# Odd layer's scan: one form of the inverse as TensorE's transpose of the other, carried products in other levels, output weights requested earlier

## The chip, the cores and the metric

One Trainium2 chip, one of its cores. The metric is the device time of one launch in microseconds (us), lower is better. The kernel runs one inference step of a two-layer backbone in float32. TensorE (PE) multiplies matrices into PSUM, VectorE (DVE) and ScalarE (ACT) work on vectors and move results from PSUM to SBUF, GpSimd (POOL) and SyncE (SP) mostly issue DMAs here.

## The reference, cut to what matters

The backbone has an even layer (mLSTM and latent attention) and an odd layer (an SSD scan and a gated delta rule, here GDN), each followed by a mixture of experts. The change touches only the scan of the odd layer and what stands just behind it:

```python
def gdn_scan(q, k, v, beta, g, S0):
    # chunked gated delta rule, log-decay gc = cumsum(g)
    amat = eye(L) + dec_strict * (kc @ kc.T) * bc          # unit lower triangular
    u0 = triangular_solve(amat, vc)
    w  = triangular_solve(amat, exp(gc) * kc)
    pmat = dec_incl * (qc @ kc.T) * bc
    def step(S, xs):
        u = u0i - wi @ S
        o = exp(gi) * (qi @ S) + pi @ u
        S = exp(gl) * S + (exp(gl - gi) * bi * ki).T @ u
        return S, o

def odd_mixer(h, P, oi, ctx):
    y = h @ P['w_in_odd'][oi]
    ...
    ys = rms_norm(ys * silu(z_s), P['ssd_norm'][oi])        # SSD output, 512 wide
    og = rms_norm(of + flip_t(ob), P['gdn_norm'][oi]) * silu(z_g)   # per head of 128
    out = concatenate([ys, og], -1) @ P['w_out_odd'][oi]
```

There are 384 tokens (128 of a prompt, 256 of a sample), in three tiles of 128; both directions are scanned, with 4 GDN heads and 8 SSD heads.

## The kernel before, in words

**Units and pairs.** `scan_units` (line 153) lists six units, a direction d and a token tile c each: (0,0), (1,0), (0,1), (1,2), (0,2), (1,1). They run in three pairs, pair 0 to pair 2; below, a and b are the two units of a pair. Pairs 1 and 2 carry a state in (`sequence`), pairs 0 and 1 hand one on (`moves_on`). All work of one unit is 128 rows by 512 columns: four heads of 128 by 128.

**The inverse.** Each unit needs the inverse of its unit triangular matrix. It is built in six levels, from blocks of one up to blocks of 64. It is kept in two forms: `XT`, and its transpose `X`. `AT` is the matrix, and `level(n)` on DVE (L2407) cuts from it the blocks `LT` of level n. In each level n of 1 to 6 (L1438 to L1482 on PE):

- `T1` = LT and X multiplied (PE, L1447 by the helper L1015), copied from PSUM to `TT` by ACT (L1820);
- `XT` product = TT and XT multiplied (PE), subtracted from `XT` by DVE (L2466);
- `XX` product = XT and TT multiplied the other way round (PE), subtracted from `X` by DVE (L2469); not in level 6, since X is not needed after it.

The helper `four` issues one product for each of four heads. The first `X` of a pair is a transpose of `XT` on PE (`X0`, L1433), copied by ACT (L1816).

**What stands between.** Between T1 and the two products of a level other work of the pair is issued: in levels 1 and 2 `Es` (the decays of the SSD part, spread by PE, L1010; exponentials on ACT, L1805) and `GB` (one product a unit, L1448); in level 3 `Y1` (SSD output of the tile itself, L1454); in level 4 `Y2` (SSD output of the carried state, L1462); in level 5 `HU` (the next SSD state, L1468); in level 6 `KS` (k times the carried GDN state) and `O2` (q times it). Behind level 6 come `U` (the solve), `O1` (output) and `SU` (next GDN state).

**Order and banks.** Each engine executes its instructions in the order in which the program writes them. `plan_jobs` (line 173) lists every PSUM user as a job, and job number modulo 8 is its bank. Thus a job waits, beside its inputs, until the job eight before it in this list has been read (`issue`, L877). PE's program has to issue the jobs in just this order.

**Buffers.** The buffers of the scan lie in four parts of 4096 words: one carved from the arena, and the three slots of the weight `ring`. Unit a has the arena part and slot 0, unit b slots 1 and 2.

**Behind the scan.** DVE multiplies the SSD sum `ysum` by its gate (L2508, `odd_sums`). ACT squares and sums it (L1835), takes a root (L1836), squares the 12 pieces of the GDN sum `ogsum` (L1839) and takes their roots (L1841). DVE scales both (L2515, L2522), PE transposes them (`mT`, L1522), ACT copies them (L1844), and `project_out` multiplies with `w_out_odd`. SP requests the two halves of `w_out_odd` (2 MB each, ring slots 1 and 2) when the first `odd_sums` is done (L583 of `load`, the DMA at L611), and behind them on its queue the small shift rows (L672) and the first experts of the next stage (L638).

## Time and profile before

| | |
|---|---|
| median of 3 runs | 1511.68 us (1505.21 to 1513.31) |
| the profiled execution's own time | 1506.36 us |
| its span, first to last instruction | 1504.2 us |
| mean granted TensorE clock | 0.940 of full |
| PE busy | 88% of the span |
| odd layer's scan, first T1 of pair 0 to O1 of pair 2 | 914.5 to 1124.0 us of the span |

The profiled execution is 5.3 us below the median; 2.2 us of its time lie outside the span. In the profile PE is TensorE's matmul side and PEld its weight loads; "[x <-DVE ...]" behind a row is the idle time ahead of it and what ended it. A float32 product of TensorE stands as two records in the trace and a transpose as one, so `four` is a group of 8 records and four transposes one of 4.

### The profile page before, as it was taken

The page shows a single profiled execution, that of the slowest core. Times are in us where ns is not written, and L with a number is a line of the kernel's source. Part 1 is how long each engine was busy: PE and PEld are TensorE (multiplying, and loading weights), DVE is VectorE, ACT ScalarE, POOL GpSimd, SP SyncE. Part 2 cuts the span into 40 slices and gives each one's busy share as a digit, 9 for nine tenths or more (in the row PEclk, how much of TensorE's full clock was granted, in tenths as well). Part 3 has the DMA queues.
Part 4 walks back from the last instruction along what each step waited for, and adds up shares of the span by engine and source line. Part 5 has one row for each costly group of instructions (what it writes and reads, how often), then busy time and mean ns, then how long its engine had stood idle before and what let it go on. Part 6 is the DMA issues. An engine that isn't in the chain of part 4 may idle for free.

```text
span 1504.2 us, 17094 instructions
## 1 busy us (share of the span) xinstructions
PE 1316.4 (88%) x6506; PEld 815.0 (54%) x6506; DVE 527.8 (35%) x1090; ACT 339.2 (23%) x724; POOL 112.3 (7%) x136
## 2 busy tenths in 40 slices
PE   6999788999998997888999997978877989987883
PEld 3554675466884333333565557878776843333332
DVE  3010473332234111011557817677662341101014
ACT  2100314333231111111336213221223311111111
POOL 2400010000001111110000000000000011111100
PEclk9999897999999999999999999999797999999997
DMA  9951666166537999997342200100007379999971
GB/s 362 332 180 58 223 152 246 68 238 240 222 139 296 390 415 418 418 417 311 122 152 72 85 0 1 29 1 1 1 18 287 137 294 411 413 418 418 417 287 63
DMA packets 80726, 329.12 MB, mean 219 GB/s; under 512 B 18383, under 2 KB 19577, under 8 KB 55936
## 3 DMA queue, kind: packets, MB, share of 16 engines
q1 hardware_dynamic: 66224, 300.54, 51.3%
q0 software_dynamic: 14416, 27.41, 5.7%
q8 instruction: 56, 0.92, 0.3%
q14 instruction: 30, 0.25, 0.0%
HBM read 320.04 MB, written 29.53 MB: 232 GB/s over the span
## 4 chain that ended last, share of the span: by engine, by line
PE 63%; DMA 15%; DVE 13%; issue 6%; ACT 2%; SPq 0%; POOL 0%; DVEq 0%; ACTq 0%; POOLq 0%
PE psum L921 20%; PE psum L1266 12%; PE psum L1015 9%; DMA arena<-in_moe_w_up 6%; PE psum L1292 5%; PE psum L947 3%; DMA wide<-in_moe_w_up 3%; DMA ring<-in_moe_w_up 3%; PE psum L1010 2%; DMA ring<-in_ada_w 2%; DVE arena L2381 2%; DVE wide L2341 1%; PE psum L890 1%; DMA arena<-h_rows,slot_token 1%; PE psum L954 1%
## 5 line engine op out<-in xcount | busy, mean ns | idle before, releaser
L921 PE MATMUL psum<-wide,ring 128*128 128x384 f32 x704 | 240.6, 502 | 3.8 <-ACT wide L1580 1.9
L921 PEld LDWEIGHTS psum<-wide,ring 128*128 128x128 f32 x704 | 165.6, 239 | 70.9 <-issue 9.5
L1266 PE MATMUL psum<-arena 128*64 128x512 f32 x480 | 151.6, 624 | 19.0 <-DMA ring<-in_moe_w_up 11.7
L1266 PE MATMUL psum<-ring,arena 128*64 128x512 f32 x384 | 134.4, 624 | 8.9 <-DMA wide<-in_moe_w_up 4.7
L1015 PE MATMUL psum<-ring 128*128 128x128 f32 x872 | 114.6, 290 | 18.0 <-issue 8.7
L1015 PEld LDWEIGHTS psum<-ring 128*128 128x128 f32 x872 | 108.9, 203 | 23.2 <-issue 13.4
L921 PE MATMUL psum<-ring,wide 128*128 128x512 f32 (+2 forms) x336 | 116.1, 507 | 0.0
L2252 DVE TENSOR_TENSOR arena<-arena,psum 128x256 f32<-128x256 f32 x34 | 14.3, 421 | 286.7 <-ACT arena L1728 286.7
L1266 PEld LDWEIGHTS psum<-arena 128*64 128x64 f32 x480 | 47.0, 144 | 96.6 <-issue 96.4
L1266 PE MATMUL psum<-wide,arena 128*64 128x512 f32 x224 | 88.1, 610 | 7.5 <-DMA arena<-in_moe_w_up 7.5
L921 PEld LDWEIGHTS psum<-ring,wide 128*128 128x128 f32 x336 | 58.3, 190 | 57.2 <-issue 56.4
L1728 ACT ACTIVATE arena<-psum 128x256 f32<-128x256 f32 x34 | 13.1, 385 | 320.7 <-PE psum L1266 320.7
L1292 PE MATMUL psum<-arena 128*64 128x512 f32 x240 | 75.1, 618 | 8.3 <-DVE arena L2256 8.3
L1266 PEld LDWEIGHTS psum<-ring,arena 128*64 128x64 f32 x384 | 42.0, 143 | 65.3 <-issue 65.3
L1292 PE MATMUL psum<-ring,arena 128*64 128x512 f32 x192 | 65.7, 598 | 6.2 <-DVE arena L2256 6.2
L2265 DVE TENSOR_SCALAR arena<-psum,share 128x512 f32<-128x512 f32 x34 | 25.5, 751 | 122.4 <-PE psum L1292 122.3
L795 POOL DMA_INDIRECT y_rows<-arena,slot_row x32 | 32.3, 1008 | 395.1 <-DVE arena L2265 381.9
L784 POOL DMA_INDIRECT arena<-h_rows,slot_token x32 | 32.7, 1021 | 356.4 <-DVE slot_token L2225 347.3
L2094 DVE SCALAR_TENSOR_TENSOR xT<-psum,modT,xT 128x128 f32<-128x128 f32 x64 | 23.7, 413 | 86.7 <-PE psum L921 76.1
L890 PE MATMUL psum<-cst 128*128 128x128 f32 (+1 forms) x236 | 52.0, 367 | 2.4 <-issue 2.4
L947 PE MATMUL psum<-ring,sil 128*32 128x512 f32 x368 | 50.5, 669 | 1.6 <-DMA ring<-in_ada_w 1.6
L2381 DVE SCALAR_TENSOR_TENSOR arena<-arena,colsT 128x388 f32<-128x388 f32 x80 | 49.8, 623 | 2.8
(505 smaller groups left out, 1717.5 us busy)
## 6 DMA issues: line engine op xcount, KB each, us to landing
ring<-in_ada_w SPq DMA_DIRECT2D x23, 2048.0 KB, 13.0
arena<-in_moe_w_gate SPq DMA_DIRECT2D x28, 1024.0 KB, 14.0
arena<-in_moe_w_up SPq DMA_DIRECT2D x28, 1024.0 KB, 20.4
arena<-in_moe_w_down SPq DMA_DIRECT2D x28, 1024.0 KB, 20.8
ring<-in_moe_w_gate SPq DMA_DIRECT2D x24, 1024.0 KB, 13.7
ring<-in_moe_w_up SPq DMA_DIRECT2D x24, 1024.0 KB, 18.8
ring<-in_moe_w_down SPq DMA_DIRECT2D x24, 1024.0 KB, 20.9
ring<-in_w_in_odd SPq DMA_DIRECT2D x7, 2048.0 KB, 8.5
```

The lines of the kernel that those rows point to most:

```text
L784: pool.indirect_dma_start(out=hrow[u], out_offset=None, in_=h_dram, in_offset=bass.IndirectOffsetOnAxis(ap=slot_token[:, n:n + 1].bitcast( ...
L795: pool.indirect_dma_start(out=y_dram[l], out_offset=bass.IndirectOffsetOnAxis(ap=slot_row[:, n:n + 1].bitcast(U32), axis=0), in_=yrow[u], ...
L890: mm(out, ident, cst[:, 0:width], start=True, stop=True)
L921: ins = mm(out, lhs(k), rhs(k), start=(k == 0), stop=(k == n - 1))
L947: ins = mm(b[at_:at_ + 32, :], sil[:, 4 * half + k, :], w[half][:, k, parity::2], start=(k == 0), stop=(k == 3), tile_position=(0, at_))
L1010: ins = mm(b[:, tok(h)], col(h).to_broadcast([P, P]), ident, start=True, stop=True)
L1015: ins = mm(b[:, h * width:(h + 1) * width], lhs(h), rhs(h), start=True, stop=True)
L1266: ins = mm(psum[half, 2 + s, :].rearrange("p (w f) -> p w f", w=2), hg[s][:, k, half], buffers[UNITS[q][h] % BUFFERS][0][:, :, k, :], star ...
L1292: ins = mm(psum[half, 5 + n, :], act_s[s][:, j, half], buffers[UNITS[q][h] % BUFFERS][1][:, j, 512 * n:512 * n + 512], start=(j == 0), sto ...
L2094: ins = stt(xT[:, m, t0:t1], bank(name, l, m)[:, t0:t1], modT[:, l, part, m, j:j + 1], xT[:, m, t0:t1], ALU.mult, ALU.add)
L2265: ts(yrow[q % 2][:, 512:D], psum[:, 6, :], share[:, q:q + 1], None, ALU.mult).then_inc(S(f"{kind}yb"), 1)
L2381: ins = stt(conv[:, i, :], cin[:, i, w:w + COUT], wcol[w], conv[:, i, :], ALU.mult, ALU.add)
```

## The change

- **X from XT.** The XX product is gone. XT is subtracted first, then PE transposes the new XT into the same PSUM job (`XX`, four transposes a unit), and ACT copies it to X. PE waits for DVE's subtraction (`taken("XT", u, n)`), ACT for PE, and the next T1 for ACT. DVE's subtraction from X is gone.
- **Order within a level.** Only Es stays between T1 and the XT product. All other work of the level stands behind the XT product and ahead of the transposes. On DVE the XT subtraction moves ahead of the other work of the level as well.
- **Levels.** KS and its right side `Rg` move from level 6 to level 3; pair 0's HU from level 5 to level 4; `ysum` times its gate from behind the scan into level 5 of pair 2.
- **Behind the scan.** ACT squares tile 0 of ogsum in level 3 of pair 2, takes its root in level 4, and squares ysum in level 6. After O1 only the squares and roots of tiles 1 and 2 are left. DVE scales ysum and tile 0 first, then tiles 1 and 2 head by head, and each head's `mT` waits for its own three pieces.
- **Buffers and weights.** What lives only until level 3 or so (G, E1, xdt, xw, EB, and Uw, AT) lies in ring slots 1 and 2, what lasts (XT, X, LT, TT, Rg, U, y2, PT) in the arena part and slot 0. SP requests the first half of w_out_odd when Y1 of pair 2 has been read, the second when the last LT has been cut.

The diff, cut to its core (the same edits in `plan_jobs` are left out, as are the loops' unchanged bodies):

```diff
-        parts = (carve(4096), ring[:, 0, :], ring[:, 1, :], ring[:, 2, :])
-        G = [parts[2 * w][:, 0:1024] for w in range(2)]
...
+        passing, lasting = (ring[:, 1, :], ring[:, 2, :]), (carve(4096), ring[:, 0, :])
+        G = [passing[w][:, 0:1024] for w in range(2)]
+        E1, xdt, xw, EB = ([passing[w][:, 512 * n:512 * n + 512] for w in range(2)] for n in range(2, 6))
+        Uw, AT = ([passing[n][:, 512 * w:512 * w + 512] for w in range(6, 8)] for n in range(2))
+        XT, X, LT, TT, Rg, U, y2, PT = ([lasting[w][:, 512 * n:512 * n + 512] for w in range(2)] for n in range(8))
...
                 if (kind, what) == ("out", (1, 0)):
-                    sp.wait_ge(S("odd_sums"), 1)
+                    for u in (4, 5):
+                        sp.wait_ge(*taken("Y1", u))
+                if (kind, what) == ("out", (1, 1)):
+                    sp.wait_ge(S("lt"), 36)
...
# TensorE, level n of a pair
+                    if n <= 2:
+                        for u, d, c in two:
+                            spread(issue("Es", u, n - 1), lambda h: cb[:, d, c, 4 * (n - 1) + h:4 * (n - 1) + h + 1])
                     for u, d, c in two:
...
+                        b = issue("XT", u, n)
+                        pe.wait_ge(*taken("T1", u, n))
+                        four(b, lambda h: TT[d][:, tok(h)], lambda h: XT[d][:, tok(h)])
+                    if n <= 2:
+                        for u, d, c in two:
                             g = n - 1
-                            spread(issue("Es", u, g), lambda h: cb[:, d, c, 4 * g + h:4 * g + h + 1])
                             ready(mm(issue("GB", u, g)[:, 0:P], conv[:, 4 + g, cols(c)], conv[:, 6 + g, cols(c)],
...
+                        if sequence:
+                            for u, d, c in two:
+                                b = issue("KS", u)
+                                if pair == 2:
+                                    pe.wait_ge(*taken("SU", u - 2))
+                                four(b, lambda h: conv[:, 12 + h, cols(c)], lambda h: Sg[:, 1, d, tok(h)])
...
-                    for u, d, c in two:
-                        b = issue("XT", u, n)
-                        pe.wait_ge(*taken("T1", u, n))
-                        four(b, lambda h: TT[d][:, tok(h)], lambda h: XT[d][:, tok(h)])
-                        if n < 6:
-                            four(issue("XX", u, n), lambda h: XT[d][:, tok(h)], lambda h: TT[d][:, tok(h)])
+                    if n < 6:
+                        for u, d, c in two:
+                            b = issue("XX", u, n)
+                            pe.wait_ge(*taken("XT", u, n))
+                            for h in range(4):
+                                ins = nc.tensor.transpose(b[:, tok(h)], XT[d][:, tok(h)], ident)
+                            ready(ins)
...
-                pe.wait_ge(S("odd_rows"), 1 if f < 4 else 2)
+                pe.wait_ge(S("odd_rows"), 1 if f < 4 else f - 2)
...
# ScalarE, the same level, and behind the scan
+                    if pair == 2 and n == 3:
+                        gdn_squares(0)
+                    if pair == 2 and n == 4:
+                        fn(ms12[:, 0:4], ms12[:, 0:4], ACT.Sqrt, scale=1.0 / DK, bias=eps[:, 0:1])
+                    if pair == 2 and n == 6:
+                        for c in range(TILES):
+                            act.wait_ge(S("odd_sums"), c + 1)
+                            done(fn(scratch, ysum[:, c, :], ACT.Square, accum_out=ms3[:, c:c + 1]), "act_own")
+                    if n < 6:
+                        for u, d, c in two:
+                            act.wait_ge(*computed("XX", u, n))
+                            take(fn(X[d], bank("XX", u, n), ACT.Copy), "XX", u, n)
...
-            done(fn(ms12, ms12, ACT.Sqrt, scale=1.0 / DK, bias=eps[:, 0:1]), "roots")
+            for u in (4, 5):
+                act.wait_ge(*taken("O1", u))
+                gdn_squares(units[u][1])
+            done(fn(ms12[:, 4:12], ms12[:, 4:12], ACT.Sqrt, scale=1.0 / DK, bias=eps[:, 0:1]), "roots")
...
# VectorE
+                    for u, d, c in two:
+                        dve.wait_ge(*computed("XT", u, n))
+                        take(tt(XT[d], XT[d], bank("XT", u, n), ALU.subtract), "XT", u, n)
...
-                        if n < 6:
-                            dve.wait_ge(*taken("X0", u))
-                            take(tt(X[d], X[d], bank("XX", u, n), ALU.subtract), "XX", u, n)
...
+                    if n == 5 and not moves_on:
+                        for c in range(TILES):
+                            done(tt(ysum[:, c, :], ysum[:, c, :], zs[:, c, :], ALU.mult), "odd_sums")
...
+            for h in range(4):
+                gated(0, h)
             dve.wait_ge(S("roots"), 4)
...
+            for h in range(4):
+                gated(1, h)
+                done(gated(2, h), "odd_rows")
```

How the instructions stand, at three places. In these rows one product is one MATMUL of 128x128, as is one transpose. TensorE in pair 1, from the first products of level 2 to the first of level 4, before (L1015 the products, L1010 Es, L1448 GB, L1454 Y1; the first row holds XT and XX of level 1 and T1 of level 2, a to b):

```order
L1015 MATMUL psum<-ring 128x128 x24
L1010 MATMUL psum<-cst,arena 128x128 x4
L1448 MATMUL psum<-arena 128x128
L1010 MATMUL psum<-cst,arena 128x128 x4
L1448 MATMUL psum<-arena 128x128
L1015 MATMUL psum<-ring 128x128 x24
L1454 MATMUL psum<-arena 128x64 x8
L1454 MATMUL psum<-ring 128x64 x8
L1015 MATMUL psum<-ring 128x128 x24
```

The same stretch with the change (L1023 the products, arena for unit a and ring for unit b; L1018 Es, L1462 GB, L1502 the transposes, L1469 Y1), from T1 of level 2:

```order
L1023 MATMUL psum<-arena 128x128 x4
L1023 MATMUL psum<-ring 128x128 x4
L1018 MATMUL psum<-cst,arena 128x128 x8
L1023 MATMUL psum<-arena 128x128 x4
L1023 MATMUL psum<-ring 128x128 x4
L1462 MATMUL psum<-arena 128x128 x2
L1502 MATMUL psum<-cst,arena 128x128 x4
L1502 MATMUL psum<-cst,ring 128x128 x4
...
L1469 MATMUL psum<-ring 128x64 x16
L1023 MATMUL psum<-arena 128x128 x8
L1502 MATMUL psum<-cst,arena 128x128 x4
```

XT and XX stood next to each other at the end of a level. Now XT stands ahead of GB and of Y1, KS (the x8 row) follows Y1, and the transposes end the level.

VectorE from level 2 to the first subtraction of level 3 in pair 1, before (L2434 Es, L2466 and L2469 the subtractions from XT and X, L2475 G, L2478 and L2479 the inputs of Y1, L2407 the blocks of a level):

```order
L2434 TENSOR_TENSOR ring<-psum,cst 128x512
L2466 TENSOR_TENSOR ring<-ring,psum 128x512
L2469 TENSOR_TENSOR ring<-ring,psum 128x512
...
L2475 TENSOR_TENSOR arena<-arena,psum 128x512
L2478 TENSOR_TENSOR arena<-arena 128x512
L2479 TENSOR_TENSOR arena<-arena 128x512
...
L2407 TENSOR_TENSOR ring<-ring,cst 128x512 x2
```

And with the change (L2477 Es, L2481 the subtraction from XT, L2488 G, L2491 and L2492 the inputs of Y1, L2451 the blocks):

```order
L2477 TENSOR_TENSOR ring<-psum,cst 128x512 x2
L2481 TENSOR_TENSOR arena<-arena,psum 128x512
L2481 TENSOR_TENSOR ring<-ring,psum 128x512
L2488 TENSOR_TENSOR ring<-ring,psum 128x512
L2491 TENSOR_TENSOR ring<-arena 128x512
L2492 TENSOR_TENSOR ring<-ring,arena 128x512
...
L2451 TENSOR_TENSOR arena<-ring,cst 128x512
L2451 TENSOR_TENSOR ring<-ring,cst 128x512
```

Two operations a level are gone, and the subtraction is the next thing that VectorE does after Es. ScalarE behind the scan, before (L1827 the copy of U, L1835 the squares of ysum, L1839 those of ogsum):

```order
L1827 ACTIVATE ring<-psum 128x512 x2
L1835 ACTIVATE arena,small<-arena 128x512 x3
L1836 ACT_TABLE_LOAD
L1836 ACTIVATE small<-small,eps 128x3
L1839 ACTIVATE arena,small<-arena 128x128 x12
L1841 ACTIVATE small<-small,eps 128x12
L1844 ACTIVATE wide<-psum 128x384 x8
```

And with the change, from level 4 of pair 2 (L1848 the copy of T1, L1864 that of X, L1860 the squares of ysum, L1834 those of ogsum):

```order
L1856 ACT_TABLE_LOAD
L1856 ACTIVATE small<-small,eps 128x4
L1864 ACTIVATE arena<-psum 128x512
...
L1860 ACTIVATE wide,small<-arena 128x512 x3
L1867 ACTIVATE arena<-psum 128x512
L1867 ACTIVATE ring<-psum 128x512
L1872 ACTIVATE small<-small,eps 128x3
L1834 ACTIVATE wide,small<-arena 128x128 x8
L1876 ACTIVATE small<-small,eps 128x8
L1879 ACTIVATE wide<-psum 128x384 x8
```

The load of the function table and the squares of ysum now stand ahead of the copy of U (L1867), and eight squares of ogsum are left behind it.

## Rows read from the trace of the kernel before

**Rows 1.** The page: span, busy time of PE, DVE and ACT.

```profile
span 1504.2 us, 17094 instructions
PE 1316.4 (88%) x6506; PEld 815.0 (54%) x6506; DVE 527.8 (35%) x1090; ACT 339.2 (23%) x724; POOL 112.3 (7%) x136
```

**Rows 2.** Busy time by stretch: start:end, length, PE, PEld, DVE, ACT, POOL, granted clock, DMA.

```profile
914.46:964.04 49.58, 44.00 (x352) 42.42 (x353) 32.97 (x48) 12.40 (x29) 0.00 (x0) 0.97 0.00 1
984.26:1040.41 56.15, 50.43 (x393) 48.33 (x393) 41.32 (x61) 12.38 (x29) 0.00 (x0) 0.96 0.00 1
1058.70:1117.75 59.05, 51.85 (x385) 50.23 (x385) 39.93 (x59) 12.39 (x29) 0.00 (x0) 0.90 0.00 1
1117.75:1123.98 6.23, 6.05 (x48) 5.79 (x48) 1.99 (x3) 1.19 (x2) 0.00 (x0) 0.73 0.01 3
1123.98:1141.77 17.79, 5.59 (x24) 4.87 (x25) 8.64 (x22) 13.01 (x42) 0.55 (x1) 0.55 0.67 236
```

**Rows 3.** Timeline, pair 0, levels 4 to 6: start, us, engine, line, operation, count [idle before].

```profile
946.65 5.69 PE L1015 MATMUL psum<-ring 128*128 128x128 f32 x48 [1.01 <-issue]
...
951.49 0.69 DVE L2466 TENSOR_TENSOR ring<-ring,psum 128x512 f32<-128x512 f32 x1 [0.38 <-PE psum L1015]
...
953.00 1.13 PE L1015 MATMUL psum<-ring 128*128 128x128 f32 x8 [0.66 <-issue]
...
961.08 3.10 PE L1015 MATMUL psum<-ring 128*128 128x128 f32 x24 [0.66 <-issue]
...
962.30 0.60 ACT L1820 ACTIVATE ring<-psum 128x512 f32<-128x512 f32 x1 [1.19 <-PE psum L1015]
...
963.04 1.13 PE L1015 MATMUL psum<-ring 128*128 128x128 f32 x8
```

**Rows 4.** Timeline of PE, eight transposes behind pair 0.

```profile
969.84 1.04 PE L1505 MATMUL psum<-cst,arena 128*128 128x128 f32 x8
```

**Rows 5.** Timeline, pair 1, the transposes of X0 and their copy.

```profile
979.19 0.63 PE L1433 MATMUL psum<-cst,ring 128*128 128x128 f32 x4 [2.08 <-DVE ring L2421]
979.85 0.60 ACT L1816 ACTIVATE ring<-psum 128x512 f32<-128x512 f32 x1 [2.40 <-PE psum L1433]
```

**Rows 6.** Timeline of PE, pair 1, T1 of b in levels 2 and 3, and Y1 of a.

```profile
996.74 1.16 PE L1015 MATMUL psum<-ring 128*128 128x128 f32 x8 [1.33 <-DVE arena L2475]
...
1006.03 1.16 PE L1015 MATMUL psum<-ring 128*128 128x128 f32 x8 [1.33 <-DVE arena L2475]
1007.57 1.97 PE L1454 MATMUL psum<-arena 128*128 128x64 f32 x16 [0.38 <-DVE arena L2479]
```

**Rows 7.** Busy time by stretch: level 3 of pair 1, of pair 2; the 42 transposes.

```profile
1006.03:1016.99 10.96, 9.71 (x81) 9.26 (x81) 9.01 (x14) 1.16 (x2) 0.00 (x0) 1.00 0.01 2
1079.15:1094.61 15.46, 14.32 (x81) 14.00 (x81) 9.01 (x14) 1.19 (x2) 0.00 (x0) 0.67 0.00 1
894.39:900.94 6.55, 4.75 (x43) 4.51 (x41) 4.02 (x7) 4.19 (x7) 1.13 (x2) 1.00 0.00 0
```

**Rows 8.** Timeline of PE, the first T1 of pair 1, both units.

```profile
984.26 3.75 PE L1015 MATMUL psum<-ring 128*128 128x128 f32 x16 [0.36 <-DVE ring L2407]
```

**Rows 9.** Timeline behind the scan: DVE, ACT, PE.

```profile
1128.98 2.08 DVE L2515 SCALAR_TENSOR_TENSOR arena<-arena,small,gain_row 128x512 f32<-128x512 f32 x3
1134.28 0.23 DVE L2518 RECIPROCAL small<-small 128x12 f32<-128x12 f32 x1 [3.23 <-ACT small L1841]
1134.54 3.24 DVE L2522 SCALAR_TENSOR_TENSOR arena<-arena,small 128x128 f32<-128x128 f32 x12
...
1128.67 0.31 ACT L1839 ACTIVATE arena<-arena 128x128 f32<-128x128 f32 x1
...
1137.93 2.79 PE L1522 MATMUL psum<-cst,arena 128*128 128x128 f32 x12 [3.94 <-DVE arena L2522]
1141.77 7.59 PE L921 MATMUL psum<-wide,ring 128*128 128x384 f32 x16 [1.05 <-ACT wide L1844]
```

**Rows 10.** Waits of SP's queue behind the scan: us in total, times, longest.

```profile
SPq L638 <- PE psum L921: 38.7, 1, 38.7
```

More of the change, by code:

```diff
@@ L1470, in _ @@
                             ready(ins)
[L1471 to L1482 removed]
+                    elif n == 6 and sequence:
+                        for u, d, c in two:
+                            four(issue("O2", u), lambda h: conv[:, 8 + h, cols(c)], lambda h: Sg[:, 1, d, tok(h)])
+                    if n < 6:
+                        for u, d, c in two:
+                            b = issue("XX", u, n)
[3 more added lines that the diff above has]
+                            ready(ins)
                 for u, d, c in two:
@@ L1807, in decays, with gdn_squares @@
                 ins.then_inc(S(name), 1)
+            scratch = skip[:, 0, :]
+            def gdn_squares(c):
+                for h in range(4):
+                    done(fn(scratch[:, 0:P], ogsum[:, c, h * P:(h + 1) * P], ACT.Square,
+                            accum_out=ms12[:, 4 * c + h:4 * c + h + 1]), "act_own")
             for pair in range(3):
@@ L2401, in first, with carried_out @@
                     return (d, c) in ((0, 0), (0, 1), (1, 2))
+                def carried_out(u, d, c):
+                    og = ogsum[:, c, :]
+                    dve.wait_ge(*computed("O2", u))
+                    dst = og if first(d, c) else y2[d]
+                    take(tt(heads(dst, 4), heads(bank("O2", u), 4), b4(ecb[:, d, c, 8:12]), ALU.mult), "O2", u)
+                    if not first(d, c):
+                        o_(tt(og, og, y2[d], ALU.add))
                 def level(n, u, d):
@@ L2429, in _ @@
                             level(n + 1, u, d)
-                    for u, d, c in two:
-                        ys, og, hs = ysum[:, c, :], ogsum[:, c, :], hsT[:, s, d, :]
-                        if n <= 2:
+                    if n <= 2:
+                        for u, d, c in two:
                             dve.wait_ge(*computed("Es", u, n - 1))
@@ L2453, in _ @@
                         elif n == 6 and sequence:
+                            carried_out(u, d, c)
+                    if n == 3 and sequence:
+                        for u, d, c in two:
                             dve.wait_ge(*computed("KS", u))
```

93 lines of the change are left out of this document (36 added, 57 removed).

## The prediction

> **What bounds the kernel now.** I read the page first: PE is busy for 88% of the span, DVE for 35%, ACT for 23% [rows 1]. This is a mean over many stages, so I cut out the stage that the change touches. The busy times by stretch [rows 2] give the three pairs of the scan from their first T1 to U: 49.58, 56.15 and 59.05 us, 164.8 together, and 17.79 us from the last sum of O1 to the first product with w_out_odd. DMA is idle in the pairs. PE is busy for 89, 90 and 88% of them, DVE for 66 to 74%, and the granted clock is near full except in pair 2 (0.90). So the pairs are bound by PE together with the hand-overs that PE waits for, and the tail by a chain over ACT and DVE (PE 5.59 of 17.79 us).
>
> The timeline of one level without other work shows the chain [rows 3]. T1 of unit b starts at 946.65 and the next one at 953.00, a period of 6.35 us. In it PE issues 48 records, then waits until DVE has made two subtractions of 0.69 us; 951.49 is their start, and 953.00 follows their end by some 0.1. The same rows give every hand-over. A group of 8 records takes 0.89 us, 0.97 behind a stall (5.69 us for 48 records with a last record's tail of 0.27). PE to DVE is 0.30 us from the end of issue (946.65 + 0.97 + 4 x 0.89 = 951.18 to 951.49). PE to ACT is 0.26 (961.08 + 0.97 to 962.30). ACT takes 0.60 us, and PE starts 0.14 after it (962.90 to 963.04). In levels 1 and 2 the period is 9.29 us (996.74 to 1006.03), and an idle time of 1.33 stands in it: T1 of b has its bank from GB of a, which DVE reads last [rows 6].
>
> **What goes and what comes.** Removed are 30 groups of XX, 0.89 us each. In their place come 30 groups of four transposes; eight transposes take 1.04 us [rows 4], less the tail 0.77 to 0.87, so 0.44 a group. That is 13.5 us less issue on PE. DVE loses 30 subtractions, ACT gains 30 copies of 0.60. The price is a longer chain: T1, ACT, XT, DVE, transpose, ACT, where the last ACT was not. Transposes at 979.19 reach ACT at 979.85 [rows 5], 0.66 us; with the copy and 0.14 the next T1 can start 1.40 us after the transposes of its unit, 1.44 taken.
>
> *A new level, units a and b, from T1 of a.* T1 0.97 + 0.89 = 1.86. The copy of a ends at 0.97 + 0.26 + 0.60 = 1.83, so XT starts at 1.97 and both end at 3.83. DVE subtracts a from 3.24 to 3.93 and b from 4.13 to 4.82. Without other work the transposes start at 4.03 and 4.92, ACT copies a from 4.77 to 5.37, and the next T1 starts at **5.51** (6.35 before). With other work of length s behind XT (s over 1.1) the transposes stand behind it, and the period is 3.83 + s + 1.44 = **5.27 + s**.
>
> *Levels 1 and 2.* Es (1.79) hides TT's copy; then XT 1.79, GB 0.45, the first transposes at 5.89: period **7.33**, against 9.29. The bank stall goes, since T1 of the next level now has the banks of Es. DVE has the most to do in level 2 (twelve operations of 0.72, 8.6 us, those for Y1 last), so it falls 1.6 us behind in level 3. Y1 stands ahead of the transposes there and covers it.
>
> *Level 3.* Y1 is 1.80 us a unit (1.97 less the tail [rows 6]), 3.60: **8.87** in pair 0. KS adds 1.79: **10.66** in pairs 1 and 2, where level 3 took 10.96 without KS [rows 7].
>
> *Levels 4 to 6.* Y2 or HU is 1.73: **7.00** where one stands, 5.51 where none does. Level 6 ends at U: **4.03** in pair 0, 1.86 + 0.11 + 1.86 + 1.79 = **5.62** with O2. U no longer waits for KS's right side.
>
> *Start of a pair.* The long DVE part ahead of the first T1 stays, and so does its low clock. Sixteen records take 3.75 there [rows 8] instead of 2.1, so 1.6 is added to level 1 in each pair.
>
> Sums: pair 0: 8.93 + 7.33 + 8.87 + 7.00 + 5.51 + 4.03 = 41.67, **7.9** saved. Pair 1: 8.93 + 7.33 + 10.66 + 7.00 + 7.00 + 5.62 = 46.54, **9.6**. Pair 2: 8.93 + 7.33 + 10.66 + 7.00 + 5.51 + 5.62 = 45.05, **14.0**. Of the last 4.5 us are clock and not work: level 3 of pair 2 took 15.46 us at a granted clock of 0.67, the same level of pair 1 10.96 at 1.00 [rows 7]. U and O1 of pair 2 ran at 0.73 [rows 2]; behind a shorter wait I take **1.0** of their 6.23 back (nothing and 1.7, which is 0.27 of it, are the ends).
>
> *Behind the scan.* From the end of O1's last sum: the squares of u = 4 ran beside it, those of u = 5 take 4 x 0.43 (twelve in 5.2 us [rows 9]) and the root 0.30, ready at about 2.9. DVE meanwhile copies and inverts (0.7), scales ysum (2.08) and tile 0 (4 x 0.27), and is free at 3.9. So DVE binds now. Reciprocal 0.25, eight pieces of 0.27 (twelve in 3.24) to 6.3, the last three of twelve transposes that took 2.79, so 0.7, the last copy and the start of the product 1.2: 8.2 us against 17.79, **9.6** saved. The table load, the squares of ysum and four of ogsum are hidden in levels 3, 4 and 6 of pair 2, where ACT has some 3 us free between its copies of TT and of X; if they weren't, they would cost 2 to 4 us.
>
> *Weights sooner.* This by itself I cost at nothing: they were requested at the start of the tail, the DMA was busy for 0.67 of it, and the product was released by ACT's copy, not by a DMA [rows 2, 9]. SP's small DMAs behind them move ahead too. The first experts then waited 38.7 us for PE again [rows 10], so earlier requests there change nothing; the stage behind follows PE and takes the saving over whole.
>
> Sum: 7.9 + 9.6 + 14.0 + 1.0 + 9.6 = 42.1 us. Y1's products are half as wide, and such a stretch with a stall ahead of it drew the low clock in one pair of three. Y1 now stands behind XT with another stall 1.4 us later, so I leave one such fall in: 42.1 - 4.5 = **37.6**. On the profiled execution's own 1506.36 this gives 1468.8. The median stands 5.3 us above it, as the clock and other chance of three runs fall; a new median may stand anywhere between, and I forecast **1470**.
>
> **A rule against the change.** The row first: 42 transposes alone (4.75 us) and 1.80 us of idle time behind them passed at a granted clock of 1.00 [rows 7]. So by this trace they hold the clock at 2.4 GHz as products do, and the sum has it so. The Trainium skill (TensorE: Matmul & The Clock Gate, Part 4: PE-mode transpose) says the opposite, that full clock doesn't engage for transposes, as they don't count as busy in the same way. It is the first rival.
>
> **The rivals.**
>
> 1. *Transposes count as idle time; slower.* Then each level ends with 0.9 us of transposes and 0.6 of waiting that look like one pause. Where the clock fell in mid-scan it cost 4.5 us [rows 7]. If all 15 levels with transposes pay it, 67.5 are lost and 42.1 won: 1532. It decides from ten falls on. Against it stand the 42 transposes; for it, that the falls at the starts of pairs come where only eight transposes run. Chance 0.05. (By the rule of the Trainium skill above it would be so; the trace does not agree.)
>
> 2. *Clock falls in every level 3, and slower hand-overs.* ACT to PE is 0.14 in one row; but behind the scan the last transposes end at 1140.72 and the product starts at 1141.77 [rows 9], 1.05 us for a copy of some 0.6, so 0.45 of hand-over. With 0.45 in place of 0.14 ahead of 15 T1 and 12 XT this is 8 us, with two more falls 9: 1486. Chance 0.12.
>
> 3. *ACT is late with X in levels 1 and 2.* Eight exponentials stand ahead of the copy; by my count they end at 6.2, and the copy is wanted at 6.6. A copy 2 us late in six levels gives back 12: 1481. Chance 0.06.
>
> 4. *The expert stage is paced by its own weights and keeps the old end in part.* SP's 38.7 us of waiting speaks against it. It would keep the tail's 9.6: 1479. Chance 0.06.
>
> 5. *More is won.* No fall in Y1, none at the starts of pairs (three times 1.6), 1459. Chance 0.06.
>
> The forecast itself has 0.65, from 1462 to 1478.
>
> **Range and chances.** 1458 to 1486 takes in cases 2 to 5 mostly and leaves 1 and the far edges out. About 0.5% (7.5 us) is what a measurement can tell from no change. Faster by more than that: all but rival 1 and a sliver, 0.93; within it 0.02; slower 0.05.
>
> **What would show it.** Right: T1 to T1 of 7.3 in levels 1 and 2 without a stall on DVE, 5.5 and 7.0 in levels 4 and 5, pairs near 42, 47 and 45 us, a tail near 8 with DVE as the last releaser. Wrong: a granted clock of half in most levels (rival 1), T1 waiting for ACT longer than 0.6 us (2, 3), or pairs as forecast with a span that shrinks by less (4).

## The result, and the profile after

The changed kernel takes **1465.82 us** (median of 4 runs, 1464.71 to 1467.7) beside 1512.49 us for the kernel before (4 runs, 1505.21 to 1514.9): ratio 0.9701, 95% interval 0.9675 to 0.9727. The profiled execution took 1467.7 us, its span is 1465.3.

The forecast was 1470. The page of the changed kernel, first the span, then busy time, share and instructions by engine:

```profile
span 1465.3 us, 16887 instructions
PE 1300.8 (89%) x6386; PEld 796.3 (54%) x6386; DVE 508.0 (35%) x1061; ACT 357.6 (24%) x755; POOL 112.3 (8%) x136
```

Against [rows 1] PE lost 120 records: 30 groups of 8 records (XX) became groups of 4 (the transposes). DVE lost 19.8 us of work, ACT gained 18.4. The share of PE hardly moved, so the page says nothing of where 39 us of span went. The stretches do, in the columns of [rows 2]: the three pairs, U with O1, and the tail, from the last sum of O1 to the first product with w_out_odd.

```profile
919.17:960.48 41.31, 40.02 (x313) 37.45 (x313) 26.11 (x38) 18.37 (x39) 0.00 (x0) 0.96 0.00 1
980.51:1026.77 46.26, 44.97 (x353) 42.58 (x354) 34.33 (x50) 18.36 (x39) 0.00 (x0) 0.96 0.01 1
1044.98:1089.87 44.89, 43.70 (x344) 41.30 (x345) 33.65 (x49) 23.74 (x55) 0.00 (x0) 0.96 0.27 95
1089.87:1094.59 4.72, 4.53 (x50) 4.16 (x48) 3.52 (x6) 2.27 (x7) 0.00 (x0) 1.00 0.01 0
1094.59:1103.42 8.83, 4.32 (x25) 3.93 (x25) 7.24 (x20) 6.88 (x23) 0.55 (x1) 0.81 0.22 70
```

PE's share of a pair rose from 88 to 90% to 97%: most of its waiting is gone, and so are 10 to 11% of its records. The saving, part by part, in us:

| | before | forecast | after | saved |
|---|---|---|---|---|
| pair 0 | 49.58 | 41.67 | 41.31 | 8.27 |
| pair 1 | 56.15 | 46.54 | 46.26 | 9.89 |
| pair 2 | 59.05 | 45.05 | 44.89 | 14.16 |
| U and O1 of pair 2 | 6.23 | 5.23 | 4.72 | 1.51 |
| tail | 17.79 | 8.2 | 8.83 | 8.96 |
| sum | | 42.1 saved | | 42.8 |

From the first T1 of pair 0 to the first product with w_out_odd it is 227.31 us before and 184.25 after. The missing 0.3 lies between the pairs.

The levels, as PE's timeline of pair 1 shows them (start, us, line, operation, records, idle time ahead; a row of L1023 with x8 is the four products of one unit; L1018 is Es, L1469 Y1, L1502 the transposes):

```profile
989.45 1.13 PE L1023 MATMUL psum<-arena 128*128 128x128 f32 x8
...
991.31 1.95 PE L1018 MATMUL psum<-cst,arena 128*128 128x128 f32 x16
...
995.33 0.60 PE L1502 MATMUL psum<-cst,arena 128*128 128x128 f32 x4
995.99 0.63 PE L1502 MATMUL psum<-cst,ring 128*128 128x128 f32 x4
996.67 1.13 PE L1023 MATMUL psum<-arena 128*128 128x128 f32 x8
...
1000.49 3.68 PE L1469 MATMUL psum<-ring 128*128 128x64 f32 x32
...
1007.25 1.13 PE L1023 MATMUL psum<-arena 128*128 128x128 f32 x8 [0.36 <-issue]
```

Level 2 is T1 to T1 from 989.45 to 996.67: 7.22 (forecast 7.33, before 9.29 [rows 6]), and the idle time of 1.33 on DVE is gone. Level 3 with KS is 996.67 to 1007.25: 10.58 (forecast 10.66). Y1 of both units stands there without the pauses of [rows 6]. Pair 0 shows a level with HU (level 4, from 944.03) and one with nothing beside it (level 5, from 950.98). ACT's rows are the copies of X of a and of b:

```profile
944.03 1.13 PE L1023 MATMUL psum<-arena 128*128 128x128 f32 x8 [0.36 <-issue]
...
947.86 1.89 PE L1491 MATMUL psum<-ring,arena 128*128 128x256 f32 x8
...
950.98 1.13 PE L1023 MATMUL psum<-arena 128*128 128x128 f32 x8 [0.36 <-issue]
...
955.74 0.60 ACT L1864 ACTIVATE arena<-psum 128x512 f32<-128x512 f32 x1 [2.04 <-PE psum L1502]
955.91 0.63 PE L1502 MATMUL psum<-cst,ring 128*128 128x128 f32 x4 [0.27 <-DVE ring L2481]
956.44 1.13 PE L1023 MATMUL psum<-arena 128*128 128x128 f32 x8
956.63 0.60 ACT L1864 ACTIVATE ring<-psum 128x512 f32<-128x512 f32 x1 [0.29 <-PE psum L1502]
```

Level 4 with HU is 6.95 (forecast 7.00), level 5 with nothing beside it 5.46 (forecast 5.51). PE is idle for 0.36 us ahead of a T1 at most; in level 5 T1 starts 0.10 us after ACT's copy of X (956.34 to 956.44).

The tail, to be read against [rows 9]:

```profile
1093.90 0.69 DVE L2530 TENSOR_TENSOR arena<-arena,psum 128x512 f32<-128x512 f32 x1 [0.20 <-PE psum L1023]
...
1097.48 4.41 PE L1543 MATMUL psum<-cst,arena 128*128 128x128 f32 x24 [3.08 <-DVE arena L2553]
1098.45 4.50 ACT L1879 ACTIVATE wide<-psum 128x384 f32<-128x384 f32 x8 [0.90 <-PE psum L1543]
1098.66 2.56 DVE L2559 SCALAR_TENSOR_TENSOR arena<-arena,small 128x128 f32<-128x128 f32 x8
1103.42 7.19 PE L929 MATMUL psum<-wide,ring 128*128 128x384 f32 x16 [1.53 <-ACT wide L1879]
```

DVE is done at 1101.22. ACT works from 1098.45 to 1102.95 on eight copies in a row, and the product follows 0.47 us later. PE's transposes start at half clock (stretches in the columns of [rows 2]):

```profile
1098.50:1099.50 1.00, 1.00 (x7) 1.00 (x6) 0.93 (x5) 0.85 (x2) 0.00 (x0) 0.50 0.00 0
1100.50:1101.89 1.39, 1.30 (x11) 0.85 (x8) 0.69 (x3) 1.33 (x3) 0.00 (x0) 1.00 0.69 262
```

Behind the tail the saving stays: from the first product with w_out_odd to the end of the span it is 362.4 us before and 361.9 after, and SP waited 45.5 us for PE ahead of the first experts, where it was 38.7 [rows 10].

```profile
SPq L646 <- PE psum L929: 45.5, 1, 45.5
```

**A draw to know of.** The scan alone gives 43.1 us, the two profiled executions differ by 38.7, and the medians by 46.7. Ahead of the scan the trace of after is 4.7 us later than that of before (first T1 at 919.17 and 914.46), in code that the change doesn't touch. Near 784 us the clock was at half for 10.2 us in the trace of after and for 3.4 in that of before. The medians differ by 3.6 us more than the scan does; no run locates these.

### The profile page after: what moved, and what is told of

The parts are those of the page before. It is cut to its first block, busy times and chain, and to the rows that moved or that the text cites. A ratio compares the mean times of both kernels' runs of the same rounds, so it can differ in the third digit from the quotient of the medians.

```text
span 1465.3 us, 16887 instructions
## 1 busy us (share of the span) xinstructions
PE 1300.8 (89%) x6386; PEld 796.3 (54%) x6386; DVE 508.0 (35%) x1061; ACT 357.6 (24%) x755; POOL 112.3 (8%) x136
## 4 chain that ended last, share of the span: by engine, by line
PE 65%; DMA 15%; DVE 11%; issue 5%; ACT 1%; SPq 0%; POOL 0%; DVEq 0%; ACTq 0%; POOLq 0%
PE psum L929 20%; PE psum L1274 12%; PE psum L1023 8%; DMA ring<-in_moe_w_up 5%; PE psum L1300 5%; DMA arena<-in_moe_w_up 4%; PE psum L955 3%; DMA wide<-in_moe_w_up 3%; PE psum L1018 2%; DMA ring<-in_ada_w 2%; DVE arena L2416 2%; DVE wide L2376 1%; PE psum L898 1%; PE psum L1257 1%; PE psum L962 1%
## 5 line engine op out<-in xcount | busy, mean ns | idle before, releaser
L1274 PE MATMUL psum<-arena 128*64 128x512 f32 x480 | 149.2, 615 | 18.7 <-DMA ring<-in_moe_w_up 13.4
L1274 PE MATMUL psum<-ring,arena 128*64 128x512 f32 x384 | 138.0, 638 | 10.5 <-DMA ring<-in_moe_w_up 5.7
L1023 PE MATMUL psum<-arena 128*128 128x128 f32 x608 | 87.4, 296 | 6.4 <-DVE arena L2021 2.6
L1023 PEld LDWEIGHTS psum<-arena 128*128 128x128 f32 x608 | 79.0, 206 | 12.5 <-issue 10.7
L1300 PE MATMUL psum<-arena 128*64 128x512 f32 x240 | 73.6, 604 | 8.3 <-DVE arena L2291 8.3
L1300 PE MATMUL psum<-ring,arena 128*64 128x512 f32 x192 | 65.7, 598 | 6.2 <-DVE arena L2291 6.2
```

Source lines behind the costliest of these rows:

```text
L1023: ins = mm(b[:, h * width:(h + 1) * width], lhs(h), rhs(h), start=True, stop=True)
L1274: ins = mm(psum[half, 2 + s, :].rearrange("p (w f) -> p w f", w=2), hg[s][:, k, half], buffers[UNITS[q][h] % BUFFERS][0][:, :, k, :], star ...
L1300: ins = mm(psum[half, 5 + n, :], act_s[s][:, j, half], buffers[UNITS[q][h] % BUFFERS][1][:, j, 512 * n:512 * n + 512], start=(j == 0), sto ...
```

## The experiments

Experiments 5, 11 and 12 are one execution each; the others are medians, with the ratio to runs of the kernel before that were timed beside them. The intervals of 2, 3, 4, 6 and 7 overlap that of the changed kernel (0.9675 to 0.9727), so the readings rest on the traces, with medians that go the same way. "First T1 to w_out_odd" is the stretch of 227.31 us before and 184.25 after.

**1. The old tail.** The squares, roots, gating and the one count for `odd_rows` go back behind the scan. The early requests for w_out_odd stay.

```diff
-                pe.wait_ge(S("odd_rows"), 1 if f < 4 else f - 2)
+                pe.wait_ge(S("odd_rows"), 1 if f < 4 else 2)
...
-                    if pair == 2 and n == 3:
-                        gdn_squares(0)
...
+            for c in range(TILES):
+                gdn_squares(c)
+            done(fn(ms12, ms12, ACT.Sqrt, scale=1.0 / DK, bias=eps[:, 0:1]), "roots")
```

> The changed kernel with everything behind the scan, and the early squares, as before (ysum times its gate, all squares and both roots behind O1; mT of the GDN part waits for all pieces). Scan, buffers and weights stay as changed. Theory (the tail is a chain over ACT and DVE of its own, worth 17.8 - 8.8 = 9.0 us): from O1's last sum to the first product with w_out_odd 17 to 18 us again, the three pairs unchanged at 41.3, 46.3 and 44.9 us, the whole 9 us above the changed kernel, near 1475. Rival (part of the old tail was waiting for the late weights or for a slow clock behind the old scan): with the weights already there the old tail takes 12 to 14 us, and the whole is 1469 to 1471.

Measured: 1475.19 us (4 runs), ratio 0.9764 (0.9729 to 0.98). Timeline of its tail, the last sum of O1 and the product:

```profile
1090.71 0.69 DVE L2521 TENSOR_TENSOR arena<-arena,psum 128x512 f32<-128x512 f32 x1 [0.21 <-PE psum L1023]
...
1109.22 7.75 PE L929 MATMUL psum<-wide,ring 128*128 128x384 f32 x16 [1.05 <-ACT wide L1873]
```

From 1091.40 to 1109.22 are 17.82 us, as before (17.79), with the weights requested early. So the early weights alone bring the tail nothing. The pairs were not quite unchanged: 41.98, 46.60 and 45.42 us, 1.5 more together, with granted clocks of 0.94 and 0.95 where after had 0.96.

**2. The product in place of the transposes.** XX is again a product on PE and a subtraction on DVE, in the new order of a level.

```diff
+                            four(issue("XX", u, n), lambda h: XT[d][:, tok(h)], lambda h: TT[d][:, tok(h)])
...
-                            for h in range(4):
-                                ins = nc.tensor.transpose(b[:, tok(h)], XT[d][:, tok(h)], ident)
...
-                            take(fn(X[d], bank("XX", u, n), ACT.Copy), "XX", u, n)
...
+                            take(tt(X[d], X[d], bank("XX", u, n), ALU.subtract), "XX", u, n)
```

> The changed kernel with X again by a product next to XT and a subtraction on DVE; the order within a level, the levels of KS and HU, banks and the tail stay as changed. Theory (a level is set by its chain and by what stands in it, and the product costs only what the longer chain over ACT gave up): level periods 7.67 in levels 1 and 2 (7.2 with transposes), 9.1 and 10.9 in level 3 (8.75 and 10.6), 7.3 with Y2 or HU (6.95), 6.35 in an empty level (5.46); 2.5, 1.9 and 2.5 us more in the three pairs, so about 7 us above the changed kernel, 1473. Rival (PE's issue time is the bound, so that the 30 products in place of 30 times four transposes cost their full 0.45 us each): 13.5 us more, 1479. Second rival (the transposes bring nothing, since the longer chain eats what they save): within 2 us of the changed kernel.

Measured: 1473.92 us, ratio 0.9744 (0.9706 to 0.9783). Its pairs:

```profile
916.40:960.19 43.79, 42.52 (x352) 41.46 (x353) 32.98 (x48) 12.40 (x29) 0.00 (x0) 0.98 0.00 1
980.41:1028.89 48.48, 47.87 (x393) 46.82 (x394) 41.19 (x60) 12.39 (x29) 0.00 (x0) 0.97 0.01 1
1047.11:1095.68 48.57, 47.30 (x385) 46.19 (x386) 40.50 (x59) 17.75 (x45) 0.00 (x0) 0.96 0.26 88
```

They are 2.5, 2.2 and 3.7 us longer than after's, 8.4 together, of which the theory had 7. By the text's price the transposes save 13.5 us of issue on PE; that the longer chain over ACT takes the other 5 back is the reading, from this difference.

**3. The old order in a level.** Transposes and ACT's copies as in the changed kernel, but Es, GB, Y1, KS, Y2, HU and O2 all stand ahead of XT, and from level 3 on DVE too subtracts from XT behind its other work of the level.

```diff
             if n <= 2:
-                jobs += [("Es", u, n - 1) for u in two]
-            jobs += [("XT", u, n) for u in two]
-            if n <= 2:
-                jobs += [("GB", u, n - 1) for u in two]
+                jobs += [(name, u, n - 1) for u in two for name in ("Es", "GB")]
...
+            jobs += [("XT", u, n) for u in two]
             if n < 6:
                 jobs += [("XX", u, n) for u in two]
...
+                    if n > 2:
+                        for u, d, c in two:
+                            dve.wait_ge(*computed("XT", u, n))
+                            take(tt(XT[d], XT[d], bank("XT", u, n), ALU.subtract), "XT", u, n)
```

> The changed kernel with the old order within a level: Es, GB, Y1, KS, Y2, HU, O2 all between T1 and the XT product, and on DVE ahead of the XT subtraction from level 3 on; X is still a transpose. Theory (the transposes at the end of a level leave nothing to hide DVE and ACT, and VectorE's work of the level now delays XT): period 7.5 in levels 1 and 2, near 12 in level 3 of pairs 1 and 2, 8 in levels 4 and 5 with Y2 or HU, Y1 stalls for its inputs by about 1.5; pairs 2 to 4, 4 to 6 and 3 to 5 us longer, together 9 to 14 us above the changed kernel, 1475 to 1480. Rival (order is nothing, the gain of the scan is that of the transposes): within 2 us of the changed kernel.

Measured: 1471.83 us, ratio 0.9745 (0.9708 to 0.9781). The pairs are 41.92, 51.25 and 49.01, so 9.7 us longer. The median is only 6.0 above the changed kernel's, below the 1475 to 1480 of the theory; 1.7 of the difference is the first 16 records of the projection, 5.53 us here and 7.19 in after, the rest is not located. The stalls that the theory had ahead of Y1 did not come. PE in pair 1, the transposes of levels 3 and 4 (L1498):

```profile
1007.32 0.63 PE L1498 MATMUL psum<-cst,arena 128*128 128x128 f32 x4 [1.17 <-DVE arena L2517]
...
1015.47 0.63 PE L1498 MATMUL psum<-cst,arena 128*128 128x128 f32 x4 [1.20 <-DVE arena L2517]
```

From the one to the other it is 8.15 us, where a level with Y2 takes 6.95 in after, and 1.20 of it is idle time ahead of the transposes. Nothing stands between XT and the transposes, so PE waits for DVE's subtraction. In pair 0 this hardly matters (0.6). The 8.4 us of the transposes and the 9.7 of the order are not the whole: together they are 18.1, and the pairs of before are 32.3 us longer than after's, 27.8 without the fall of the clock. The rest lies in what both experiments keep (the levels of KS and HU, the banks) and in how the two halves work together; no run parts these.

**4. Weights late.** The changed kernel with the request for w_out_odd behind O1, as before.

```diff
                     for u in (4, 5):
-                        sp.wait_ge(*taken("Y1", u))
+                        sp.wait_ge(*taken("O1", u))
```

> The changed kernel with w_out_odd requested only when O1 of pair 2 has been read, as late as before. The prediction had the earlier request at nothing. Theory now (nothing was right beside the old tail of 17.8 us, but the new one is 8.8 us long and the two loads need 10 to 12): the first product waits for a DMA, starts 2 to 4 us later, and its releaser in the trace is the load of w_out_odd; 1468 to 1470. Rival (the first half is enough to start and the second lands beside the first products, run at the low clock): within 1 us of the changed kernel.

Measured: 1471.33 us (1467.62 to 1481.54), ratio 0.9756 (0.9705 to 0.9807); with this spread the trace has to decide. Timeline of the tail, SP's queue and PE. Then the time from issue to landing of the two requests, here and in the kernel before, and POOL's request in the stretch (KB, us to landing):

```profile
1091.40 0.95 SPq L619 DMA_DIRECT2D ring<-in_w_out_odd  x2
...
1106.01 7.64 PE L929 MATMUL psum<-wide,ring 128*128 128x384 f32 x16 [6.42 <-DMA ring<-in_w_out_odd]
```

```profile
DMA to landing us min/median/max: 7.9/10.9/13.9
DMA to landing us min/median/max: 7.8/10.1/12.5
gain_row<-in_norm_final POOLq DMA_DIRECT2D x1, 512.0 KB, 7.3
```

The tail (1091.33 to 1106.01) is 14.68 us, 5.85 longer than after's, and the product is released by the DMA. The second half, issued at 1091.9, lands 13.9 us later, at 1105.8, and the product waits for both halves. The theory's 2 to 4 took 10 to 12 us for the two, where it is the later one that counts. POOL's gain row of 512 KB is under way beside them; what it costs them was not tried. With experiment 1 this gives the tail for all four combinations: 17.79 with neither edit, 17.82 with early weights alone, 14.68 with the reordered work alone, 8.83 with both.

**5. The kernel before, once more.**

> The kernel before, once more, for its trace alone. The profiled execution of before had the granted clock at half for 10.2 us from level 3 of pair 2 on, which made that level 4.5 us longer; none of five traces of kernels with the new scan has the clock down between the first products of a pair and its U. Theory (chance of where the pause ahead of Y1 falls): this trace may have such a stretch in no pair or in another one; level 3 then takes 10.9 to 11.3 us in pairs without it, and the scan from the first T1 of pair 0 to U of pair 2 is near 199 us instead of 203.3. Rival (the old order draws the low clock in pair 2 every time): the same stretch again, level 3 of pair 2 at 15.5 us.

Measured: one execution, 1507.74 us. Pair 2's level 3 took 10.96 us this time, and the clock fell in level 3 of pair 0 instead, for 10.2 us. From the first T1 to w_out_odd it was 227.51 us.

**6 and 7. PE kept at work ahead of a pair.** Where PE waits for DVE ahead of the first transposes of X, it issues transposes (18 and 26) or products (9 and 13) of constants into the bank that these transposes will overwrite.

```diff
                     b = issue("X0", u)
+                    for _ in range(9 if d == 0 else 13):
+                        mm(b[:, 0:P], ident, cst[:, C_UP:C_UP + P], start=True, stop=True)
                     pe.wait_ge(S("xt_first"), u + 1)
```

> The changed kernel with the waits of TensorE at the start of each pair filled: 18 transposes of a constant ahead of X0 of unit a and 26 ahead of that of unit b, into the bank that X0 then overwrites; 1.97 and 2.84 us at 0.11 each. In the changed kernel the clock is at half for 6.8 us there, and the first two T1 take 3.6 us instead of 1.9. Theory (transposes hold the clock as products do; 42 of them did): granted clock 1.00 through all three starts, first T1s 1.9 us, 1.6 us less per pair, 4 to 5 us below the changed kernel, near 1461. Rival (a rule by which transposes don't count as work for the clock): clock at half as before, the transposes then take twice as long and delay X0 by up to 2 us a pair: 1466 to 1472.

> The same with 9 and 13 products of 128 columns in place of 18 and 26 transposes, 2.0 and 2.9 us. Theory: the same clock and the same time as with transposes, 1461. Rival (only products count): clock 1.00 here and half in the run with transposes, 3 to 8 us between the two.

Measured: 1456.84 us with transposes, ratio 0.9649 (0.9612 to 0.9685), and 1456.73 with products, 0.964 (0.9601 to 0.9679). Both are some 4 us below the 1461 of the theory. The start of pair 0 with transposes (L1440), on PE, and the stretches 907.87 to 910.87 and 913 to 916 of it, with the granted clock in front of the last two columns:

```profile
907.87 3.00 PE L1440 MATMUL psum<-cst 128*128 128x128 f32 x26
...
912.53 1.13 PE L1023 MATMUL psum<-arena 128*128 128x128 f32 x8 [0.88 <-DVE arena L2453]
913.50 1.06 PE L1023 MATMUL psum<-ring 128*128 128x128 f32 x8
```

```profile
907.87:910.87 3.00, 3.00 (x28) 2.77 (x26) 2.86 (x5) 0.60 (x1) 0.00 (x0) 1.00 0.00 0
913.00:916.00 3.00, 3.00 (x29) 3.00 (x29) 1.94 (x4) 1.19 (x2) 0.00 (x0) 1.00 0.00 0
```

In the changed kernel the first T1 of a pair take nearly twice as long, at half the clock; here those of pair 1 (those of pair 0 took 2.05 and 1.87):

```profile
980.51 2.04 PE L1023 MATMUL psum<-arena 128*128 128x128 f32 x8 [0.36 <-DVE arena L2451]
982.35 1.91 PE L1023 MATMUL psum<-ring 128*128 128x128 f32 x8
```

From the first T1 to w_out_odd it is 179.40 us with transposes and 178.98 with products, 4.9 and 5.3 below after, 1.4 to 1.9 of it a pair. The medians fell by 9.0 and 9.1. Another 1.7 is seen in the first 16 records of the projection (5.53 us, 7.19 in after), where nothing was filled; the rest is not located. X0 of b follows X0 of a after 3.62 us with and without the transposes, so the filling did not hold it up.

**8. A DVE product out of the way.** Kernel 7, with DVE's two products for PT (0.72 us each) behind the tiles of level 1, and 10 filling products for unit b.

```diff
+                for u, d, c in two:
+                    level(1, u, d)
+                for u, d, c in two:
                     dve.wait_ge(*computed("KQ", u))
                     take(tt(PT[d], EB[d], bank("KQ", u), ALU.mult), "KQ", u)
-                for u, d, c in two:
-                    level(1, u, d)
```

> The kernel with products ahead of the first transposes of each pair, and DVE's product for PT moved behind the tiles of level 1 that release the first T1. Two of them (0.72 us each) stood ahead of those tiles, on the path by which PE waits for the first T1. Theory: DVE is what the first T1 waits for, so each pair starts 1.4 us sooner, 4.3 us in the three pairs; ratio to the filled kernel about 0.997 (1452.5 us). The bank of PT comes free later, but Es asks for it only behind T1: at most 0.3 us of wait in a pair. Rival: the bank or PT itself (needed by the products of level 3) is late and takes it back: 0, pairs as long as before from the first transposes to U, 1456.7 us.

Measured: 1453.99 us (1451.89 to 1465.64, 5 runs), ratio 0.9616 (0.9576 to 0.9655). From T1 to T1 of neighbouring pairs it is 58.33 and 61.69 us, where kernel 7 has 59.66 and 62.75: 1.3 and 1.1 a pair, where the theory had 1.4. The median is 2.7 below kernel 7's (4.3 expected), and the intervals overlap.

**9. The same ahead of the projection.** Kernel 8 with 13 more products ahead of the transposes behind the scan.

```diff
+                if f == 0:
+                    for _ in range(13):
+                        mm(b[:, 0:P], ident, cst[:, C_UP:C_UP + P], start=True, stop=True)
```

> The kernel of the run before it, with 13 more products into the bank of the first transposes behind the scan, ahead of these transposes, where PE is idle. Theory: the clock is then full in the first product with w_out_odd: its 16 rows take 5.5 us instead of up to 7.2, and the time is 0 to 1.7 us shorter (nothing where the clock was already up there). Rival: the filling products delay the transposes, as the last of their operands is there before the filling ends: 0.5 to 1.5 us longer.

Measured: 1454.92 us, ratio 0.961 (0.9572 to 0.9647), so no difference to kernel 8 that can be told. In kernels 6, 7 and 8 the first 16 records of the projection already took 5.53 us, as here.

**10. The filling in the kernel before.** The same 9 and 13 products in the kernel before the change.

> The kernel before, with 9 or 13 products into the bank of the first transposes of each pair, where PE waits for DVE. Theory: the gain of such products has nothing to do with the change: eight T1 groups at a pair's start pass at full clock, 1.6 us a pair, some 5 us in all; ratio 0.9965 (about 1505). Falls of the clock at Y1 stay as they were, by chance. Rival: what the filled kernels won (9 us, where 4.9 are seen in the scan) belongs to another effect of the new order: then nothing or under 2 us here.

Measured: 1502.92 us (1496.25 to 1509.03, 10 runs), ratio 0.993 (0.9903 to 0.9957): 10.6 us, between 6.5 and 14.7, twice what the theory had. The trace shows 222.54 us from the first T1 to w_out_odd, 4.8 less than before, with a fall of the clock in Y1 of pair 2:

```profile
1079.31 1.16 PE L1015 MATMUL psum<-ring 128*128 128x128 f32 x8 [1.33 <-DVE arena L2477]
1080.85 2.83 PE L1456 MATMUL psum<-arena 128*128 128x64 f32 x16 [0.39 <-DVE arena L2481]
1083.47 3.62 PE L1456 MATMUL psum<-ring 128*128 128x64 f32 x16
...
1094.76 1.13 PE L1015 MATMUL psum<-ring 128*128 128x128 f32 x8 [0.76 <-issue]
```

**11 and 12. Kernels 10 and 8, one more execution each.**

> One more look at the kernel before with the filling products. Its runs were 10.6 us faster (6.5 to 14.7) where its trace shows 4.8 in the scan. Theory: the rest is chance of the clock in Y1: a fall there costs 4.5 us and comes in some runs (1 in each of the two traces without the filling and 1 in the one with it); then this trace has 222.5 us from the first T1 to the first product with w_out_odd if a fall is in it and 218 if none is. Rival: the filling saves more in the scan than the eight T1 groups at each pair's start: under 218 with a fall in it.

> One more look at the kernel with the filling products and the later product for PT, whose profiled run (1465.6 us) was 11.7 us over its median. Theory: the excess lies ahead of the scan and behind it, as low clock by chance; here again 176.5 us from the first T1 to the first product with w_out_odd, and a first T1 nearer 912 to 918 than 923.5. Rival: the order itself makes a slow stretch ahead of the scan: first T1 at 923 again, in a run of the median's time.

Measured for 11: 1497.01 us, 216.65 us from the first T1 to w_out_odd and no fall in any Y1. The same rows:

```profile
1075.94 1.16 PE L1015 MATMUL psum<-ring 128*128 128x128 f32 x8 [1.33 <-DVE arena L2477]
1077.48 1.97 PE L1456 MATMUL psum<-arena 128*128 128x64 f32 x16 [0.38 <-DVE arena L2481]
1079.65 1.97 PE L1456 MATMUL psum<-ring 128*128 128x64 f32 x16 [0.20 <-DVE ring L2481]
...
1086.90 1.13 PE L1015 MATMUL psum<-ring 128*128 128x128 f32 x8 [0.66 <-issue]
```

So one kernel passes with and without the fall, with the same pauses ahead of Y1: from T1 of b in level 3 to T1 of b in level 4 it is 15.45 us (1079.31 to 1094.76) with it and 10.96 (1075.94 to 1086.90) without. Measured for 12: 1456.01 us, 176.86 us from the first T1 to w_out_odd, the first T1 at 915.02 where the profiled run of kernel 8 had it at 923.54. Of the 9.6 us by which that run was longer, 8.5 lay ahead of the scan and 1.4 behind the start of the projection.

## Why the prediction was right

**The pairs.** Right in each part. Levels measured 7.22, 10.58, 6.95 and 5.46 where the text had 7.33, 10.66, 7.00 and 5.51. The chain that was added up from hand-overs of [rows 3] and [rows 5] is 0.05 to 0.11 us too long a level. Of 31.5 us forecast for the pairs 32.3 came. Experiments 2 and 3 show that both halves of the change are needed: with the product 8.4 us are lost in the pairs, with the old order 9.7. U with O1 gave 1.51 us, at a granted clock of 1.00, where the text took 1.0.

**One leftover fall of the clock, 4.5 us.** Not needed in this run. In the traces of kernels with transposes or the new order (after, 1 to 4, 6 to 9, 12) no Y1 passed at a low clock, 30 passes in all; in the old order with the pauses ahead of Y1 it was 3 of 12 (before, 5, 10, 11). If the three falls were spread over the 42 passes at random, all would land in those 12 about once in 50 times (an estimate from these counts). The pauses are what differs between [rows 6] and the new rows. Kernel 3 has Y1 at its old place but had none of those pauses, and no fall either. That the pauses bring the falls is the likeliest reading; no run put them back alone. With the fall taken out, the sum was 42.1, and the scan gave 43.1.

**Start of a pair.** Right: the low clock stayed (3.75 us for sixteen records [rows 8], 3.75 again from 980.51 to 984.26), and the 1.6 a pair that the text put on it is what kernels 6 and 7 won in the scan.

**The tail.** Nearly right, 0.6 us too short. The text had DVE as the last to bind. DVE was done 6.63 us after O1's last sum (6.3 in the text). From there to the product it took 2.20 (1.9 in the text), with ACT as the last: its eight copies of 0.49 us stand in a row of 4.50 that ends 1.7 after DVE, and the text counted only the last one of them. The row starts late, as the first transposes ran at a granted clock of 0.50. In kernel 3 they ran at full clock (twelve in 1.50 us), ACT's last copy waited for PE alone, and the tail was 8.35.

**"Weights sooner", costed at nothing.** This step failed, though the sum did not show it. The text argued from the tail of before, where the product waited for ACT's copy. There the second half had landed at 1137.7 (12.5 us after its issue), 4 us ahead of the product. It priced the request by the old tail, though those 12.5 us do not fit into the 8.2 that it forecast. Beside the old tail it is worth nothing (experiment 1); beside the new one it is worth 5.9 us (experiment 4), since the later half takes 13.9 us to land. The reordered work alone gives 3.1 of the tail's 9.0 us. The sum came out because the change has both edits.

**Rivals.** The first, transposes as idle time, falls: outside the starts of pairs no level with transposes ran at a low clock, and kernel 6 holds the clock at 2.4 GHz (granted 1.00) through waits filled with nothing but transposes. Slow hand-overs: ACT to PE took 0.10 us in level 5 and 0.47 ahead of the product with w_out_odd, so the 0.45 belongs to that product and not to the levels; no. ACT late in levels 1 and 2: the copy was there, 7.22. Experts paced by weights: no, 362.4 and 361.9 us from the product to the end, and SP waited longer than before, 45.5 us. More won: half of its case came true, no fall in Y1; the starts stayed.

**The number.** 1470 was made on the profiled execution's 1506.36 with 37.6 saved. The median of before is 6.1 above that run, and 46.7 was saved by the medians. From that median the text's 37.6 would give 1474.9, 9 us too high: 4.5 for the fall that was left in, 1.0 for parts that gave more than priced, and 3.6 that no run locates. That the forecast missed by only 4 us is in part luck, as the low base made up for half of it.

## What to carry to other kernels

Price a load that is moved ahead against the stage as the other edits leave it, not as it was: a transfer hidden by a slow stage comes out when the stage shrinks. In a chain over three engines, issue the independent products just behind the one whose result is fetched; the same instructions in another order were worth 9.7 us in the pairs here (6.0 by the medians). Where TensorE waits 2 to 3 us for VectorE ahead of dense work, try cheap products into a bank that is about to be overwritten: here they kept its clock up, and the traces show no cost.

## What the runs showed of the hardware

- **Transposes hold the clock, and it rises under them.** With 18 and 26 float32 transposes as the only filling the granted clock was 1.00 and the next T1 took 1.1 us a group instead of 2.0, as with products (1456.84 and 1456.73 us). In the tail of after PE did nothing but transposes from 1097.48 to 1101.89, and the granted clock went from 0.50 to 1.00 within them. The Trainium skill (TensorE: Matmul & The Clock Gate, Part 4: PE-mode transpose) says that full clock doesn't engage for them; this case's runs do not agree.
- **A fall comes in some executions and not in others.** The same kernel (10 and 11) passed level 3 of pair 2 in 15.45 and in 10.96 us. A single execution can stand 4.5 us off by one such fall.
- **Filling gave more than its place shows.** In the kernel before it brought 10.6 us (6.5 to 14.7) by the medians, 4.8 in the scan of one trace and 10.7 in that of the other, which had no fall. That the filling makes falls in Y1 rarer is possible; two traces don't settle it.
- **The fastest version** is kernel 8 with 1453.99 us (kernel 9 is not to be told from it), ratio 0.9616 to the kernel before and some 12 us below the changed kernel.
